# A decoder layer with product-key experts: 24 first-layer tiles beside the gate matrix, 64 in a stage of their own, outputs summed in groups of four

## The chip, the cores and the metric

The program runs on one core of one Trainium2 chip. The metric is the device time of one execution in microseconds (us), the median of the runs; lower is better. The engines of the core are TensorE (PE; PEld is its loading of weights), VectorE (DVE), ScalarE (ACT), GpSimd (POOL) and SyncE (SP). DMA queues are named by the engine that issues them.

## The reference

One inference step of one layer, for 1024 prompt tokens and 32 sample tokens with D = 1024: three mixers (window attention, gated linear attention, attention into a memory), merged by gates, and then the expert layer, which is all that the change touches:

```python
def one_block(xb):                                   # tokens after RMSNorm
    q = (xb @ wq).reshape(P_BLOCK, P_HEADS, 2, half)  # 8 heads
    s1, s2 = q[:, :, 0] @ k1.T, q[:, :, 1] @ k2.T     # 128 keys each
    v1, i1 = top_k(s1, 16); v2, i2 = top_k(s2, 16)
    sc, sel = top_k(v1 + v2 (all pairs), 16)
    eidx = the 16 chosen of i1 * 128 + i2             # of 16384 experts
    gate = softmax(sc)
    hid = einsum('thkd,td->thk', u_tab[eidx], xb)
    return einsum('thk,thkd->td', gelu(hid) * gate, v_tab[eidx])
```

So y = h + sum over 8 x 16 chosen experts of gate * gelu(u . x) * v, in float32.

## The kernel before

Tokens are held transposed, features on the 128 partitions. The first 256 of the 1056 tokens (`TG`) are computed sparsely: for each of the 2 x 128 pairs of a token tile and a choice, GpSimd gathers 128 rows of u (and later of v) by an indirect DMA, and VectorE multiplies and sums (u), or multiplies and adds (v): 512 row jobs. The other 800 tokens (`TD`) are computed densely over all 16384 experts: 128 tiles of 128 experts. For each tile the hidden values are u times x, then GELU, times a gate that is zero for experts that were not chosen, and then v is applied and added to `m.x2`. Each float32 product is made of three float32r products (`exact_product`, L70: high x high, high x low, low x high), so each operand is first rounded by ScalarE (high) and the rest taken by VectorE (low). A tile's 800 tokens are two halves of 400 columns.

The last stages in order:

- `choose_experts` (L1458): queries, scores, the best 16 by VectorE; beside it TensorE already computes the hidden values of 40 of the 128 tiles (`KEPT`), which go to DRAM (`kept`).
- `build_gate_matrix` (L1715): for 100 groups of 8 tokens, the gates of all experts: VectorE makes one-hot rows (`hot2` L1783, `hot1` L1787), GpSimd weights six of the eight tokens (L1800) and ScalarE two (L1828), TensorE multiplies (L1816), ScalarE copies out (L1837), and SyncE stores a block of four groups (32 tokens, 2 MB) to DRAM (L1859). PSUM banks 0 to 3 are used.
- `run_experts` (L1864): 64 groups of two tiles. Groups 0 to 19 use kept hidden values; from group 20 on TensorE computes the hidden values of two tiles (`hidden_products`, L1961, for the group after) and the outputs of two (`output_products`, L1974) in turn. Per group SyncE loads the gates (`x_g`), kept values, v and u; ScalarE and VectorE split them; VectorE weighs (`weigh`, L2083), and adds each of 16 output sums from PSUM to `m.x2` (`add_output`, L2100, L2106). The row jobs (L2123 for u, L2126 for v) stand between in VectorE's order, one per group in the first 19 groups and some 11 in the later ones, with six row buffers for the gathers (L2064).
- `store_output` (L2172).

All orders are written out by hand, as the programs of the engines; semaphores tie them. A `Block` ends when all engines have ended it.

Of the kernel before, what the change touches and what calls it, by code (L numbers as in the profile page):

```python
# [5 lines left out]
F32 = mybir.dt.float32  # L6
# [34 lines left out]
KEPT = 40  # L41
GR = 2
# [1415 lines left out]
def choose_experts(nc, m, d, sem):  # L1458
# [13 lines left out]
    turns[TURNS] = [("u", x) for x in range(e, KEPT)]  # L1472
    jobs = [("q", 0)] + [job for turn in turns for job in turn]
    with ExitStack() as ctx:
# [14 lines left out]
        cand = sb("pcand", [P, NT, TOPK, TOPK])  # L1489
        best = sb("pbest", [P, NT, TOPK])  # L1490
        expo = sb("pexpo", [P, NT, TOPK])
# [11 lines left out]
        with nc.Block() as block:  # L1503
# [75 lines left out]
            def _(act):  # L1579
# [53 lines left out]
                for x in kept_stored:  # L1633
                    act.wait_ge(x, 16 * (KEPT // 2))

# [79 lines left out]
def build_gate_matrix(nc, m, d, sem):  # L1715


    with ExitStack() as ctx:
        def sb(name, shape, dt=F32):
# [8 lines left out]
        out = sb("gm_out", [P, 2, NK, TBG])  # L1728

        turned, t_kept, hot1_made, hot2_made, weighted, last_weighted, used, copied = (  # L1730
            sem(f"gm_{x}") for x in
            ("turned", "kept", "hot1_made", "hot2_made", "weighted", "last_weighted", "used", "copied"))
        stored = [sem("gm_stored0"), sem("gm_stored1")]
        srcs = (m.e1, m.e2, m.gate)
        iota = m.const[:, C_IOTA:C_IOTA + NK]
        turns = [(s, t) for s in range(3) for t in range(GT, NT)]
        with nc.Block() as block:

            @block.tensor
            def _(pe):  # L1740
                for u, (s, t) in enumerate(turns):
                    r = tile_rows(t)
                    if u >= 8:
                        pe.wait_ge(t_kept, u - 7)
                    pe.transpose(m.ps[:, u % 8, 0:r], srcs[s][0:r, t, :],
                                 m.const[0:r, C_ID:C_ID + r]).then_inc(turned, 1)

            @block.scalar
            def _(act):
                for u, (s, t) in enumerate(turns):  # L1750
                    r, a = tile_rows(t), (t - GT) * P
                    act.wait_ge(turned, u + 1)
                    act.copy(turned_in[s][:, a:a + r], m.ps[:, u % 8, 0:r]).then_inc(t_kept, 1)
# [8 lines left out]

        GROUPS = TBG // G8
        BLOCKS = TD // TBG
        with nc.Block() as block:

            def all_groups(eng, group):
                group(0, True, 0)
                group(1, True, 1)
                with eng.Fori(1, TD // G8 // 2) as i:  # L1770
                    group(2 * i, False, 0)
                    group(2 * i + 1, False, 1)


            @block.vector
            def _(dve):
                def group(g, first, q):
                    cols = bass.ds(G8 * g, G8)
                    if not first:
# [5 lines left out]
                    if not first:  # L1785
# [4 lines left out]

                all_groups(dve, group)

            @block.gpsimd
            def _(pool):
                def group(g, first, q):
                    cols = bass.ds(G8 * g, G8 - 2)
                    pool.wait_ge(hot2_made, g + 1)
                    if not first:
# [5 lines left out]
                all_groups(pool, group)  # L1804

# [642 lines left out]
```

## Time and profile before

| | us |
|---|---|
| median of 3 runs (4488.6 to 4491.19) | 4489.08 |
| the profiled execution's own time | 4497.05 |
| its span, first to last instruction | 4495.3 |
| TensorE busy | 3944.2 (88%) |
| VectorE busy | 2847.1 (63%) |
| ScalarE busy | 1203.8 (27%) |
| GpSimd busy | 1113.1 (25%) |

The profile is one execution. Times in it count from the span's start. A busy TensorE is one with a matmul in flight; an engine's idle time costs something only where the others wait for it. The granted clock is a share of TensorE's full 2.4 GHz, so 0.50 is 1.2 GHz.

### The profile page before, as it was taken

To read this page: it belongs to the slowest core of one execution; us is meant where nothing else is said; L and a number is where in the kernel's file an instruction comes from. 1 tells how busy PE (TensorE), PEld (TensorE's weight loads), DVE (VectorE), ACT (ScalarE), POOL (GpSimd) and SP (SyncE) were. 2 spreads that over 40 slices of the span, in tenths; PEclk is the share of its full clock that TensorE was granted. 3 is DMA by queue.
4 is the path that set the end of the run, shared out by engine and by line. 5 is a ranking of instruction groups with operands and counts; after the bars stand their busy time and mean duration, and the time that the engine had idled before them with its cause. 6 is when DMAs were issued, how large, how long until landed. Compare 5 with 4: busy or idle time off the path is not lost. (4 is left out here: it accounts for less than half of the span.)

```text
span 4495.3 us, 58255 instructions
## 1 busy us (share of the span) xinstructions
PE 3944.2 (88%) x21975; PEld 3709.1 (83%) x21975; DVE 2847.1 (63%) x5001; ACT 1203.8 (27%) x1885; POOL 1113.1 (25%) x696
## 2 busy tenths in 40 slices
PE   4799884769999699999766599999999999999998
PEld 2698573558888599999655599999999999999998
DVE  2000345342222368787999788887788888778887
ACT  2112334121111222222588512222222222222221
POOL 0001000000000222222477400144434434334442
PEclk8899876579999799999999899999999999999999
DMA  2211100011112012222233566677777787777775
GB/s 98 59 41 36 58 23 19 21 40 43 43 43 74 30 61 77 74 77 82 84 159 149 213 186 181 190 238 245 244 234 252 253 251 243 239 248 246 246 251 184
DMA packets 366054, 622.15 MB, mean 138 GB/s; under 512 B 224241, under 2 KB 235425, under 8 KB 361907
## 3 DMA queue, kind: packets, MB, share of 16 engines
q1 hardware_dynamic: 285915, 334.56, 23.6%
q0 software_dynamic: 73728, 268.47, 18.1%
q10 hardware_dynamic: 6240, 16.99, 1.0%
q8 instruction: 89, 1.46, 0.1%
q14 instruction: 82, 0.67, 0.0%
HBM read 542.33 MB, written 78.12 MB: 138 GB/s over the span
## 5 line engine op out<-in xcount | busy, mean ns | idle before, releaser
L73 PE MATMUL ps<-x_act_high,x_v_high 128*128 128x400 f32 x2048 | 709.7, 347 | 53.8 <-DVE x_v_low L2080 28.6
L74 PE MATMUL ps<-x_act_low,x_v_high 128*128 128x400 f32 x2048 | 705.2, 344 | 0.0
L75 PE MATMUL ps<-x_act_high,x_v_low 128*128 128x400 f32 x2048 | 704.5, 344 | 0.0
L2106 DVE TENSOR_TENSOR xn<-xn,ps 128x400 f32<-128x400 f32 x1024 | 543.0, 562 | 51.4 <-PE ps L75 51.1
L2064 POOL DMA_INDIRECT x_rows<-in_u_rows,row_of x256 | 326.5, 1275 | 788.3 <-DVE x_row_hid L2123 736.0
L73 PE MATMUL ps<-hd_high,x_u_high 128*128 128x400 f32 x1408 | 484.8, 344 | 0.0
L74 PE MATMUL ps<-hd_low,x_u_high 128*128 128x400 f32 x1408 | 482.9, 343 | 0.0
L75 PE MATMUL ps<-hd_high,x_u_low 128*128 128x400 f32 x1408 | 481.9, 342 | 0.0
L2064 POOL DMA_INDIRECT x_rows<-in_v,row_of x256 | 335.5, 1310 | 472.3 <-DVE xn L2126 426.5
L73 PEld LDWEIGHTS ps<-x_act_high,x_v_high 128*128 128x128 f32 x2048 | 385.6, 188 | 66.0 <-DVE xn L2106 36.9
L74 PEld LDWEIGHTS ps<-x_act_low,x_v_high 128*128 128x128 f32 x2048 | 385.2, 188 | 0.0
L75 PEld LDWEIGHTS ps<-x_act_high,x_v_low 128*128 128x128 f32 x2048 | 384.7, 188 | 0.1
L2126 DVE SCALAR_TENSOR_TENSOR xn<-x_rows,x_row_hid,xn 128x1024 f32<-128x1024 f32 x256 | 328.2, 1282 | 2.3
L73 PE MATMUL ps<-hd_high,wq_high 128*128 128x400 f32 x896 | 309.8, 346 | 17.1 <-ACT kept_act L1597 17.1
L1816 PE MATMUL ps<-gm_wgt,gm_hot 128*128 128x128 f32 x1600 | 206.0, 282 | 134.9 <-ACT gm_out L1837 127.7
L2010 ACT CAST x_v_high<-x_v_raw 128x1024 fp32r<-128x1024 f32 x128 | 132.5, 1049 | 688.3 <-DMA x_v_raw<-in_v 688.3
L1816 PEld LDWEIGHTS ps<-gm_wgt,gm_hot 128*128 128x128 f32 x1600 | 187.6, 193 | 153.2 <-ACT gm_out L1837 148.6
L74 PE MATMUL ps<-hd_low,wq_high 128*128 128x400 f32 x896 | 308.8, 345 | 0.0
L2123 DVE CUSTOM_DVE_ANT_1 x_rows<-x_rows,xn 128x1024 f32<-128x1024 f32 x256 | 307.9, 1218 | 0.0
L75 PE MATMUL ps<-hd_high,wq_low 128*128 128x400 f32 x896 | 307.6, 343 | 0.0
L73 PE MATMUL ps<-x_high_again,w_spare 128*128 128x352 f32 x768 | 269.9, 351 | 38.8 <-DVE x_low L1368 30.5
L2080 DVE TENSOR_TENSOR x_v_low<-x_v_raw,x_v_high 128x1024 fp32r<-128x1024 f32 x128 | 156.3, 1221 | 215.4 <-ACT x_v_high L2010 215.0
(335 smaller groups left out, 7702.0 us busy)
## 6 DMA issues: line engine op xcount, KB each, us to landing
x_v_raw<-in_v SPq DMA_DIRECT2D x128, 512.0 KB, 5.2
gates<-gm_out SPq DMA_DIRECT2D x25, 2048.0 KB, 6.3
x_g<-gates SPq DMA_DIRECT2D x64, 800.0 KB, 8.9
x_u_raw<-in_u SPq DMA_DIRECT2D x88, 512.0 KB, 4.3
wq_raw<-in_u SPq DMA_DIRECT2D x40, 512.0 KB, 3.2
kept<-kept_act ACTq DMA_DIRECT2D x40, 400.0 KB, 2.4
x_act<-kept SPq DMA_DIRECT2D x40, 400.0 KB, 4.2
wg_raw<-in_w_m SPq DMA_DIRECT2D x24, 512.0 KB, 3.6
```

The lines of the kernel that those rows point to most:

```text
L73: pe.matmul(out, w[0], x[0], start=first, stop=False)
L74: pe.matmul(out, w[0], x[1], start=False, stop=False)
L75: return pe.matmul(out, w[1], x[0], start=False, stop=last)
L1816: mm = pe.matmul(m.ps[:, 2 * q + b, i * P:i * P + P], hot1[:, q, 4 * b + i, :], wgt[:, q, 4 * b + i, :], start=True, stop=True)
L2010: sc.copy(v_high[:, g % 2, i], v_raw[:, g % 2, i]).then_inc(v_highs, 1)
L2064: pool.indirect_dma_start(rows[:, s % ROWS, :], None, src, bass.IndirectOffsetOnAxis(ap=m.row_of[:, t, k:k + 1], axis=0)).then_inc(row_loa ...
L2080: dve.tensor_tensor(v_low[:, g % 2, i], v_raw[:, g % 2, i], v_high[:, g % 2, i].bitcast(F32), ALU.subtract).then_inc(v_lows, 1)
L2106: dve.tensor_tensor(dst, dst, m.ps[:, 4 + x % 4, 0:DC], ALU.add).then_inc(added, 1)
L2123: dve.tensor_tensor_reduce(row, row, m.n_rows[t], 1.0, 0.0, ALU.mult, ALU.add, hid[:, t, k:k + 1]).then_inc(row_used, 1)
L2126: dve.scalar_tensor_tensor(m.y_rows[t], row, hid[:, t, k:k + 1], m.y_rows[t], ALU.mult, ALU.add).then_inc(row_used, 1)
```

## The change

The 88 tiles that `run_experts` computed go to two other places, and `run_experts` is replaced. `build_gate_matrix` computes 24 tiles: after each group's eight products TensorE does a quarter of a tile (12 matmuls, PSUM banks 4 to 7), so that a block of four groups holds one tile; u is loaded by SyncE between the stores of the gates, rounded by ScalarE, and its rest is taken by VectorE. The loops there are written out. A new stage `finish_hidden` computes the other 64 tiles, with three buffers for u and four row jobs per tile beside them (256 of 512). A new stage `add_outputs` takes all 128 tiles from DRAM in 32 groups of four: each output sum is accumulated over four tiles in PSUM before VectorE adds it, in eight banks instead of four, and eight row jobs stand in each group. `gather_rows` and `row_job` are the gathers and row jobs of before as functions. The row buffers lie where the choice of experts held its results.

```diff
-KEPT = 40
-GR = 2
+EARLY = 40
+BESIDE = 24
+GR = 4
+ROWS = 6
+ROWS_BESIDE = 4
...
+        u_raw = sb("gm_u_raw", [P, 2, KT, P])
+        u = (sb("gm_u_high", [P, 2, KT, P], F32R), sb("gm_u_low", [P, 2, KT, P], F32R))
+        hid = m.spare[:, 0:2 * TD].rearrange("p (i t) -> p i t", i=2)
...
+            @block.sync
+            def _(sp):
+                for n in range(2):
+                    sp.dma_start(u_raw[:, n], d["u"][EARLY + n]).then_inc(u_loaded[n], 16)
...
+        PER = TBG // G8
+        GROUPS = TD // G8
...
+                def rest_u(n):
+                    dve.wait_ge(u_high, n + 1)
+                    dve.tensor_tensor(u[1][:, n % 2], u_raw[:, n % 2], u[0][:, n % 2].bitcast(F32),
+                                      ALU.subtract).then_inc(u_low, 1)
+                rest_u(0)
+                for g in range(GROUPS):
+                    q, cols = g % 2, slice(G8 * g, G8 * g + G8)
+                    if g >= 2:
                         dve.wait_ge(weighted, g - 1)
                         dve.wait_ge(last_weighted, g - 1)
                     dve.tensor_tensor(hot2[:, q], iota2[:], key2[:, cols].unsqueeze(1).broadcast_to([P, NK, G8]),
                                       ALU.is_equal).then_inc(hot2_made, 1)
+                    if g >= 2:
                         dve.wait_ge(used, 2 * (g - 1))
                     dve.tensor_tensor(hot1[:, q], iota.unsqueeze(1).broadcast_to([P, G8, NK]),
                                       key1[:, cols].unsqueeze(2).broadcast_to([P, G8, NK]),
                                       ALU.is_equal).then_inc(hot1_made, 1)
+                    if g % PER == 1 and g // PER + 1 < BESIDE:
+                        rest_u(g // PER + 1)
...
+                def quarter(n, i):
+                    c = i // 2
+                    a, z = HALVES[c]
+                    if i == 0:
+                        pe.wait_ge(u_low, n + 1)
+                    if i % 2 == 0 and n >= 2:
+                        pe.wait_ge(gelu_done, 2 * (n - 2) + c + 1)
+                    for k in range(4 * (i % 2), 4 * (i % 2) + 4):
+                        mm = exact_product(pe, m.ps[:, 4 + 2 * (n % 2) + c, 0:DC], [x[:, n % 2, k, :] for x in u],
+                                           [x[:, k, a:z] for x in m.hd], k == 0, k == KT - 1)
+                    if i % 2:
+                        mm.then_inc(hidden, 1)
+                for g in range(GROUPS):
+                    q = g % 2
                     pe.wait_ge(hot1_made, g + 1)
                     pe.wait_ge(weighted, g + 1)
                     pe.wait_ge(last_weighted, g + 1)
                     for b in range(2):
+                        if g >= 2:
                             pe.wait_ge(copied, 2 * (g - 2) + b + 1)
                         for i in range(4):
                             mm = pe.matmul(m.ps[:, 2 * q + b, i * P:i * P + P], hot1[:, q, 4 * b + i, :],
                                            wgt[:, q, 4 * b + i, :], start=True, stop=True)
                         mm.then_inc(used, 1)
+                    if g // PER < BESIDE:
+                        quarter(g // PER, g % PER)
...
+                def weigh(g):
                     act.wait_ge(hot2_made, g + 1)
+                    if g >= 2:
+                        act.wait_ge(used, 2 * (g - 1))
                     for i in (G8 - 2, G8 - 1):
+                        ins = act.activation(wgt[:, g % 2, i], hot2[:, g % 2, :, i], ACT.Copy,
+                                             scale=gate[:, G8 * g + i:G8 * g + i + 1])
                     ins.then_inc(last_weighted, 1)
+                def copy_out(g):
+                    blk = g // PER
+                    if g % PER == 0 and blk >= 2:
                         act.wait_ge(stored[blk % 2], 16 * (blk // 2))
+                    for b in range(2):
+                        at = G8 * (g % PER) + 4 * b
+                        act.wait_ge(used, 2 * g + b + 1)
+                        act.copy(out[:, blk % 2, :, at:at + 4].rearrange("p n t -> p t n"),
+                                 m.ps[:, 2 * (g % 2) + b, :].rearrange("p (t n) -> p t n", t=4)).then_inc(copied, 1)
+                def round_u(n):
+                    act.wait_ge(u_loaded[n % 2], 16 * (n // 2 + 1))
+                    if n >= 2:
+                        act.wait_ge(hidden, 2 * (n - 1))
+                    act.copy(u[0][:, n % 2], u_raw[:, n % 2]).then_inc(u_high, 1)
+                def gelu(n, c):
+                    a, z = HALVES[c]
+                    act.wait_ge(hidden, 2 * n + c + 1)
+                    if n >= 2:
+                        act.wait_ge(kept_stored[n % 2], 16 * (n // 2))
+                    act.activation(hid[:, n % 2, a:z], m.ps[:, 4 + 2 * (n % 2) + c, 0:DC], ACT.Gelu).then_inc(gelu_done, 1)
+                def keep(n):
+                    act.wait_ge(gelu_done, 2 * n + 2)
+                    act.dma_start(d["kept"][EARLY + n], hid[:, n % 2]).then_inc(kept_stored[n % 2], 16)
+                round_u(0)
+                weigh(0)
+                for g in range(GROUPS):
+                    n = g // PER
+                    if g + 1 < GROUPS:
+                        weigh(g + 1)
+                    copy_out(g)
+                    if g % PER == 0:
+                        if n + 1 < BESIDE:
+                            round_u(n + 1)
+                        if 1 <= n <= BESIDE:
+                            gelu(n - 1, 1)
+                    if g % PER == 1 and 1 <= n <= BESIDE:
+                        keep(n - 1)
+                    if g % PER == 2 and n < BESIDE:
+                        gelu(n, 0)
+                for x in kept_stored:
+                    act.wait_ge(x, 16 * (BESIDE // 2))
             @block.sync
             def _(sp):
+                for blk in range(TD // TBG):
+                    if 2 <= blk + 1 < BESIDE:
+                        sp.wait_ge(u_low, blk)
+                        sp.dma_start(u_raw[:, (blk + 1) % 2], d["u"][EARLY + blk + 1]).then_inc(u_loaded[(blk + 1) % 2], 16)
+                    sp.wait_ge(copied, 2 * PER * (blk + 1))
                     sp.dma_start(d["gates"][blk], out[:, blk % 2]).then_inc(stored[blk % 2], 16)
...
+def gather_rows(pool, m, d, r, first, upto):
+    for s in range(first, min(upto, len(r.jobs))):
+        kind, t, k = r.jobs[s]
+        if s >= ROWS:
+            pool.wait_ge(r.used, s - ROWS + 1)
...
+def row_job(dve, m, r):
...
+def finish_hidden(nc, m, d, sem, r):
+    FIRST, RING = EARLY + BESIDE, 3
+    COUNT = NK - FIRST
...
+            @block.sync
+            def _(sp):
+                for n in range(COUNT):
+                    if n >= RING:
+                        sp.wait_ge(hidden, 2 * (n - RING) + 2)
+                    sp.dma_start(u_raw[:, n % RING], d["u"][FIRST + n]).then_inc(u_loaded[n % RING], 16)
+            @block.tensor
+            def _(pe):
+                for n in range(COUNT):
+                    pe.wait_ge(u_lows, n + 1)
+                    for c, (a, z) in enumerate(HALVES):
+                        if n >= 4:
+                            pe.wait_ge(gelu_done, 2 * (n - 4) + c + 1)
+                        for k in range(KT):
+                            mm = exact_product(pe, m.ps[:, 2 * (n % 4) + c, 0:DC], [x[:, n % RING, k, :] for x in u],
+                                               [x[:, k, a:z] for x in m.hd], k == 0, k == KT - 1)
+                        mm.then_inc(hidden, 1)
+            @block.scalar
+            def _(act):
+                def round_u(n):
+                    if n < COUNT:
+                        act.wait_ge(u_loaded[n % RING], 16 * (n // RING + 1))
+                        act.copy(u_high[:, n % RING], u_raw[:, n % RING]).then_inc(u_highs, 1)
+                for n in range(RING - 1):
+                    round_u(n)
+                for n in range(COUNT):
+                    round_u(n + RING - 1)
+                    if n >= 2:
+                        act.wait_ge(kept_stored[n % 2], 16 * (n // 2))
+                    for c, (a, z) in enumerate(HALVES):
+                        act.wait_ge(hidden, 2 * n + c + 1)
+                        act.activation(hid[:, n % 2, a:z], m.ps[:, 2 * (n % 4) + c, 0:DC], ACT.Gelu).then_inc(gelu_done, 1)
+                    act.wait_ge(gelu_done, 2 * n + 2)
+                    act.dma_start(d["kept"][FIRST + n], hid[:, n % 2]).then_inc(kept_stored[n % 2], 16)
+                    row_gelus(act, m, r, ROWS_BESIDE * n, ROWS_BESIDE * n + ROWS_BESIDE)
+                for x in kept_stored:
+                    act.wait_ge(x, 16 * (COUNT // 2))
+            @block.gpsimd
+            def _(pool):
+                gather_rows(pool, m, d, r, 0, ROWS_BESIDE * COUNT + ROWS)
+            @block.vector
+            def _(dve):
+                def rest_u(n):
+                    if n < COUNT:
+                        dve.wait_ge(u_highs, n + 1)
+                        dve.tensor_tensor(u_low[:, n % RING], u_raw[:, n % RING], u_high[:, n % RING].bitcast(F32),
+                                          ALU.subtract).then_inc(u_lows, 1)
+                for n in range(RING - 1):
+                    rest_u(n)
+                for n in range(COUNT):
+                    for i in range(ROWS_BESIDE):
+                        row_job(dve, m, r)
+                        if i == 0:
+                            rest_u(n + RING - 1)
...
+def add_outputs(nc, m, d, sem, r):
+    GROUPS = NK // GR
+    OUT = 2 * KT
+    start = r.done
+    left = len(r.jobs) - start
+    upto = [start + left * (g + 1) // GROUPS for g in range(GROUPS)]
...
+            @block.sync
+            def _(sp):
+                def load_gates(g):
+                    if g:
+                        sp.wait_ge(gated, GR * g)
+                    src = bass.AP(tensor=d["gates"].tensor, offset=g * GR * TBG,
+                                  ap=[[NK * TBG, P], [NK * NK * TBG, TD // TBG], [1, GR * TBG]])
+                    sp.dma_start(gates[:].rearrange("p b i t -> p b (i t)"), src).then_inc(g_loaded, 16)
+                for g in range(GROUPS):
+                    load_gates(g)
+                    if g >= 2:
+                        sp.wait_ge(multiplied, OUT * (g - 1))
+                    for n in range(GR * g, GR * g + GR):
+                        sp.dma_start(act_raw[:, g % 2, n % GR], d["kept"][n]).then_inc(a_loaded[n % (2 * GR)], 16)
+                    for n in range(GR * g, GR * g + GR):
+                        sp.dma_start(v_raw[:, g % 2, n % GR], d["v"][n]).then_inc(v_loaded[n % (2 * GR)], 16)
+            @block.tensor
+            def _(pe):
+                def output_products(g, p, first):
+                    for x in range(OUT):
+                        j, (a, z) = x // 2, HALVES[x % 2]
+                        if not (first and x < 8):
+                            pe.wait_ge(added, OUT * g + x - 7)
+                        for i in range(GR):
+                            if x == 0:
+                                pe.wait_ge(act_lows, GR * g + i + 1)
+                                pe.wait_ge(v_lows, GR * g + i + 1)
+                            mm = exact_product(pe, m.ps[:, x % 8, 0:DC], [y[:, p, i, j * P:j * P + P] for y in v],
+                                               [y[:, p, i, a:z] for y in split], i == 0, i == GR - 1)
+                        mm.then_inc(multiplied, 1)
+                output_products(0, 0, True)
+                with pe.Fori(0, (GROUPS - 2) // 2) as i:
+                    output_products(2 * i + 1, 1, False)
+                    output_products(2 * i + 2, 0, False)
+                output_products(GROUPS - 1, 1, False)
+            @block.scalar
+            def _(sc):
...
+                for g in range(GROUPS):
+                    for n in range(GR * g, GR * g + GR):
+                        round_act(n)
+                    for n in range(GR * g, GR * g + GR):
+                        round_v(n)
+                    if g:
+                        row_gelus(sc, m, r, upto[g - 2] if g >= 2 else start, upto[g - 1])
+            @block.gpsimd
+            def _(pool):
+                gather_rows(pool, m, d, r, start + ROWS, len(r.jobs))
+            @block.vector
+            def _(dve):
...
+                def add_output(g, x):
+                    j, (a, z) = x // 2, HALVES[x % 2]
+                    dst = m.x2[:, j, TG + a:TG + z]
+                    if g:
+                        dve.wait_ge(added, OUT * (g - 1) + x + 1)
+                    dve.wait_ge(multiplied, OUT * g + x + 1)
+                    dve.tensor_tensor(dst, dst, m.ps[:, x % 8, 0:DC], ALU.add).then_inc(added, 1)
+                for n in range(GR):
+                    weigh(n)
+                for n in range(GR):
+                    rest_act(n)
+                for n in range(GR):
+                    rest_v(n)
+                after = {3: (weigh, 0), 4: (weigh, 1), 5: (weigh, 2), 6: (weigh, 3), 7: (rest_act, 0), 8: (rest_act, 1),
+                         9: (rest_act, 2), 10: (rest_act, 3), 11: (rest_v, 0), 12: (rest_v, 1), 13: (rest_v, 2),
+                         14: (rest_v, 3)}
+                for g in range(GROUPS):
+                    for x in range(OUT):
+                        add_output(g, x)
+                        if x in after and g + 1 < GROUPS:
+                            what, i = after[x]
+                            what(GR * (g + 1) + i)
+                        if (x < 4 or x % 2) and r.done < upto[g]:
+                            row_job(dve, m, r)
+                    while r.done < upto[g]:
+                        row_job(dve, m, r)
+                assert r.done == len(r.jobs)
...
+                r = row_sums(nc, m, sem)
+                finish_hidden(nc, m, d, sem, r)
+            add_outputs(nc, m, d, sem, r)
         store_output(nc, m, d, sem)
```

## Rows read from the trace of the kernel before

**Rows 1.** Stretches: length; PE, PEld, DVE, ACT, POOL busy; clock; DMA share; GB/s.

```profile
2187.00:2535.00 348.00, 205.97 (x1600) 187.56 (x1600) 336.07 (x200) 278.23 (x400) 256.81 (x100) 0.99 0.36 151
2572.00:2890.00 318.00, 318.00 (x1745) 317.98 (x1746) 277.18 (x438) 65.23 (x72) 16.90 (x18) 1.00 0.62 181
2890.00:4482.00 1592.00, 1565.88 (x8547) 1554.02 (x8545) 1300.15 (x1803) 334.01 (x441) 638.28 (x487) 1.00 0.76 240
```

**Rows 2.** One turn of the gate stage in order of time (start, us, engine).

```profile
2302.17 2.05 PE L1816 MATMUL ps<-gm_wgt,gm_hot 128*128 128x128 f32 x16 [1.32 <-ACT gm_out L1837]
...
2302.79 2.55 POOL L1800 TENSOR_TENSOR gm_wgt<-gm_hot,gm_gate 128x768 f32<-128x768 bf16 x1 [0.82 <-DVE gm_hot L1783]
2303.53 1.91 ACT L1837 COPY gm_out<-ps 128x512 f32 x2
2303.58 2.31 DVE L1783 TENSOR_TENSOR gm_hot<-gm_iota,gm_key 128x1024 bf16<-128x1024 bf16 x1
...
2306.15 2.57 POOL L1800 TENSOR_TENSOR gm_wgt<-gm_hot,gm_gate 128x768 f32<-128x768 bf16 x1 [0.81 <-DVE gm_hot L1783]
```

**Rows 3.** Start of the gate stage in order of time.

```profile
2187.04 0.69 DVE L1783 TENSOR_TENSOR gm_hot<-gm_iota,gm_key 128x1024 bf16<-128x1024 bf16 x1 [4.97 <-PEq L1737]
...
2190.62 5.40 PE L1816 MATMUL ps<-gm_wgt,gm_hot 128*128 128x128 f32 x32 [4.40 <-POOL gm_wgt L1800]
```

**Rows 4.** DMA issues of the page: count, KB each, median us to landing.

```profile
gates<-gm_out SPq DMA_DIRECT2D x25, 2048.0 KB, 6.3
...
wq_raw<-in_u SPq DMA_DIRECT2D x40, 512.0 KB, 3.2
kept<-kept_act ACTq DMA_DIRECT2D x40, 400.0 KB, 2.4
...
out_y<-xn SPq DMA_DIRECT2D x1, 3200.0 KB, 10.0
...
out_y_rows<-xn SPq DMA_DIRECT2D x2, 512.0 KB, 11.2
```

**Rows 5.** DMA queue of SyncE from 1700 to 2100: packets, MB, share of 16 engines.

```profile
q1 hardware_dynamic: 5328, 19.40, 14.4%
```

**Rows 6.** Groups of the expert stage, 2536 to 4482: busy us, mean ns.

```profile
L2106 DVE TENSOR_TENSOR xn<-xn,ps 128x400 f32<-128x400 f32 x1024 | 543.0, 562 | 51.4 <-PE ps L75 51.1
...
L2126 DVE SCALAR_TENSOR_TENSOR xn<-x_rows,x_row_hid,xn 128x1024 f32<-128x1024 f32 x256 | 328.2, 1282 | 2.3
...
L2080 DVE TENSOR_TENSOR x_v_low<-x_v_raw,x_v_high 128x1024 fp32r<-128x1024 f32 x128 | 156.3, 1221 | 215.4 <-ACT x_v_high L2010 215.0
L2010 ACT CAST x_v_high<-x_v_raw 128x1024 fp32r<-128x1024 f32 x128 | 132.5, 1049 | 688.3 <-DMA x_v_raw<-in_v 688.3
```

**Rows 7.** Short stretches after gaps of TensorE; the third last number is the clock.

```profile
555.00:556.00 1.00, 0.49 (x1) 0.18 (x2) 0.00 (x0) 0.00 (x0) 0.00 (x0) 0.61 1.03 393
...
2180.00:2181.00 1.00, 0.00 (x0) 0.00 (x0) 0.46 (x2) 0.00 (x0) 0.00 (x0) 0.50 0.00 0
2190.00:2193.00 3.00, 2.38 (x11) 2.41 (x12) 3.00 (x3) 1.15 (x3) 2.37 (x2) 0.50 0.00 0
```

**Rows 8.** TensorE's first matmul after a gap, with its idle time before.

```profile
555.51 1.06 PE L765 MATMUL ps<-sm_k,features 128*32 128x512 f32 x1 [3.15 <-DMA sm_k<-in_mem_k]
...
2181.04 3.47 PE L1745 MATMUL ps<-const,e 128*128 128x128 f32 x14 [4.08 <-PEq L1503]
```

**Rows 9.** Stretches of the expert stage; the last two numbers are DMA share and GB/s.

```profile
2541.00:2551.00 10.00, 0.00 (x0) 0.00 (x0) 3.73 (x4) 1.99 (x3) 1.62 (x2) 0.50 1.03 408
3000.00:4200.00 1200.00, 1180.12 (x6450) 1171.77 (x6449) 981.99 (x1384) 256.28 (x339) 496.00 (x379) 1.00 0.78 246
```

**Rows 10.** Start and end of the expert stage in order of time.

```profile
2534.80 0.37 SPq L1932 DMA_DIRECT2D x_g<-gates  x1
...
2555.64 0.70 PE L73 MATMUL ps<-x_act_high,x_v_high 128*128 128x400 f32 x1 [28.58 <-DVE x_v_low L2080]
...
4481.05 0.57 DVE L2106 TENSOR_TENSOR xn<-xn,ps 128x400 f32<-128x400 f32 x1 [0.52 <-PE ps L75]
```

More of the change, by code:

```diff
@@ L1471, in choose_experts @@
             e += 1
-    turns[TURNS] = [("u", x) for x in range(e, KEPT)]
+    turns[TURNS] = [("u", x) for x in range(e, EARLY)]
     jobs = [("q", 0)] + [job for turn in turns for job in turn]
@@ L1855, in _ @@
+                for x in kept_stored:
+                    act.wait_ge(x, 16 * (BESIDE // 2))
             @block.sync
             def _(sp):
-                for blk in range(BLOCKS):
-                    sp.wait_ge(copied, 2 * GROUPS * (blk + 1))
+                for blk in range(TD // TBG):
[3 more added lines that the diff above has]
+                    sp.wait_ge(copied, 2 * PER * (blk + 1))
@@ L2190, in row_jobs, with row_sums @@
     return jobs + [("v", 0, k) for k in range(NK - 8, NK)] + [("v", 1, k) for k in range(NK)]
+def row_sums(nc, m, sem):
+    r = Mem()
+    r.jobs = row_jobs()
+    r.first_v = [next(s for s, (kind, i, _) in enumerate(r.jobs) if kind == "v" and i == t) for t in range(GT)]
+    r.last_u = [max(s for s, (kind, i, _) in enumerate(r.jobs) if kind == "u" and i == t) for t in range(GT)]
+    r.last_of = [None] * GT
+    r.done = 0
+    r.loaded = [sem(f"row_loaded{i}") for i in range(ROWS)]
+    r.used, r.gelu, r.gated = (sem(f"row_{x}") for x in ("used", "gelu", "gated"))
+    return r
@@ new lines, in row_gelus @@
+def row_gelus(act, m, r, first, upto):
+    for t in range(GT):
+        if first <= r.last_u[t] < upto:
+            act.wait_ge(r.used, r.last_u[t] + 1)
+            act.activation(m.row_hid[:, t], m.row_hid[:, t], ACT.Gelu).then_inc(r.gelu, 1)
+def row_job(dve, m, r):
+    s, hid = r.done, m.row_hid
+    kind, t, k = r.jobs[s]
+    row = m.rows[:, s % ROWS, :].rearrange("p (a c) -> p a c", c=TG)
+    if s in r.first_v:
+        dve.wait_ge(r.gelu, t + 1)
+        dve.tensor_tensor(hid[:, t], hid[:, t], m.row_gate[:, t], ALU.mult).then_inc(r.gated, 1)
+        dve.wait_ge(r.gated, t + 1)
+    if r.last_of[t] is not None and kind == "v":
+        dve.wait_ge(r.used, r.last_of[t] + 1)
+    dve.wait_ge(r.loaded[s % ROWS], 16 * (s // ROWS + 1))
+    if kind == "u":
+        dve.tensor_tensor_reduce(row, row, m.n_rows[t], 1.0, 0.0, ALU.mult, ALU.add,
+                                 hid[:, t, k:k + 1]).then_inc(r.used, 1)
+    else:
+        dve.scalar_tensor_tensor(m.y_rows[t], row, hid[:, t, k:k + 1], m.y_rows[t], ALU.mult,
+                                 ALU.add).then_inc(r.used, 1)
+        r.last_of[t] = s
+    r.done += 1
@@ L2411 @@
 }
[L2412 removed]
+SCRATCH = {"skew": (8, P, EXT), "gates": (TD // TBG, NK, NK, TBG), "kept": (NK, P, TD)}
 def declare(nc, arrays):
```

413 lines of the change are left out of this document (86 added, 327 removed).

## The prediction

> **What bounds the kernel now.** I first read the busy time of each engine by stage, because the change touches only the last three stages [rows 1]. While the gate matrix is built (2187 to 2535 us), TensorE is busy 206 of 348 us. In the expert stage behind it TensorE is the bound: 318 of 318 us up to 2890, then 1566 of 1592. So TensorE time there is worth its full length, and 142 us of it lie idle in the gate stage.
>
> The matmul price: 1745 matmuls fill 318.00 us, 0.1822 us each [rows 1]. One tile of first-layer work is 8 x 3 x 2 = 48 matmuls, 8.745 us. One tile of output work is also 48.
>
> Next, what paces the gate stage: one turn of it in time order [rows 2]. A group of eight tokens takes TensorE 2.05 us (16 instructions), yet a turn is 3.36 us, from one weighting of GpSimd to the next. The weighting lasts 2.55 us; VectorE's `hot2`, which takes 0.69 us when GpSimd is idle [rows 3], is drawn out to 2.31 us beside it and ends 0.55 us behind it (2305.89 after 2305.34); the next weighting starts 0.26 us later.
>
> **Part 1: 24 tiles beside the gate matrix.** 24 x 8.745 = 209.9 us leave the TensorE-bound stage. In the gate stage a group becomes 2.05 + 12 x 0.1822 = 4.24 us of TensorE, 16.96 us for a block of four, longer than the four turns' 13.4. If nothing else bound, the stage would grow by 24 x (16.96 - 13.44) = 84 us only.
>
> Something else does bind. Per block, SyncE issues the 2 MB store of the gates and right behind it, on the same queue, the load of the next block's u. The store takes 6.3 us to land; a 512 KB load with nothing ahead of it 3.2 us [rows 4]. What a load does behind a store is seen at the end of the kernel: the two 512 KB stores behind the 3.2 MB one land 11.2 us after their issue, about a transfer each behind the 10.0 us of the first, so a queue is served in order [rows 4]. A 512 KB load costs 14.4% of 400 us over 38 loads = 1.52 us of the DMA engines [rows 5] (the window holds 29 u loads and 9 query loads). So u lands 6.3 + 1.55 = 7.9 us after a block's last copy. Bounds: 3.2 us (no queueing) and 6.3 + 3.2 = 9.5 (it starts when the store has landed); the row of the two stores is nearest to 7.9.
>
> Who waits? ScalarE's `round_u(n+1)` stands in its program right behind the copies of a block's first group, and VectorE's `rest_u(n+1)` behind the second group's `hot1`. Both are in-order, so behind them wait `weigh`, `hot2` of the third group, GpSimd's weighting and TensorE. The next block's u is issued only after this block's last copy, so this is a closed ring: u lands 7.9; round 1.05 and rest 1.2 (1024 columns, as for v [rows 6]); `hot2` alone 0.69 [rows 3]; weighting 2.55 and 0.2 of hand-overs; TensorE's third group 2.05, its quarter 2.19, fourth group 2.05; until the second bank of it is copied 1.2 more (two copies take 1.91 from the first bank's end [rows 2]). Sum 21.1 us for a block, against 16.96. TensorE idles for 21.1 - 17.0 = 4.1 us in each.
>
> That idling has its own price. An idle stretch of 3.15 us left the clock at half (0.61 in the microsecond of the restart), one of 4.08 us too (0.50 before its end) [rows 7, 8]. After a restart the clock stays at 0.50 for about 3 us, and the first two gate groups took 5.40 us instead of 2 x 2.05 [rows 3, 7]: 1.3 us more, and the third group lies on the ring. Ends: 0 (the clock stays) to 1.6. I take 1.4, since 4.1 us is as long as the longer of the two gaps that lost the clock: 22.5 us a block. The Trainium skill, TensorE: Matmul & The Clock Gate, section "HAM oscillation", speaks against this change: short bursts of matmuls with a DMA wait between them fall back to the slow clock at every wait. The rows agree so far; by that rule the result is the 4472 below, without it 22 x 1.4 = 31 us less, 4441.
>
> The ring holds for blocks 1 to 22. Block 0 has its loads early (17.6, its second weighting 0.6 late), block 23 loads none (17.0), block 24 has no tiles (3 x 3.36 and 3.3 to its last copy); ahead stand 5.7 us (round, rest, `hot2`, weighting, hand-overs), behind 6.6 (last store, next stage). Sum: 5.7 + 17.6 + 495.0 + 17.0 + 13.4 + 6.6 = 555.3 us against 2534.8 - 2187.0 = 347.8. The gate stage loses 207.5, about all of the 209.9 that it takes over.
>
> VectorE's 24 rests and ScalarE's 24 rounds, 48 GELUs and 24 store issues add some 4 us to a block on ScalarE and VectorE together; they fit into the 22.5 and cost nothing beyond the ring. The loop written out costs nothing that the trace shows: the stage before it is written out too.
>
> **Part 2: 64 tiles in a stage of their own.** TensorE: 64 x 8.745 = 559.7 us. Under it VectorE has four row jobs and a rest, at most 4 x 1.28 + 1.22 = 6.3 of 8.75 us [rows 6]. A tile moves four gathers, one u load (512 KB each) and a 400 KB store: 3.03 MB in 8.745 us = 347 GB/s, 40% above the 246 GB/s that the expert stage moved at a DMA share of 0.78 [rows 9]. That would be 315 GB/s at a full share, 9.62 us a tile. But 408 GB/s were moved over 10 us while gathers, v and u loads ran together [rows 9]; at that rate 7.43 us. The mix is nearest to the 408, which is of the same gathers and loads: u is asked for two tiles ahead (17.5 us) and six gathers are in flight. I take 5 us of waiting in all; ends 0 and 64 x 0.88 = 56. Around it: first u 4.5, round and rest 2.3, hand-overs 0.4, half clock 1.5 at the start; last GELUs 1 and the wait for the last stores 2.4 [rows 4], stage change 1. Sum 559.7 + 13.1 + 5 = 577.8.
>
> **Part 3: outputs in groups of four.** The 128 output tiles stay 6144 matmuls, 1119.4 us. What goes is half of VectorE's additions: 512 x 0.562 = 288 us [rows 6], but that was beside a TensorE that stood still for 26 of 1592 us only; what can be won is that and the start. VectorE per group of four: 16 x 0.56 + 8 x 0.95 (L2080's by columns) + 4 x 1.22 + 8 x 1.28 = 31.7 of TensorE's 35.0 us, and eight banks let it lag by 17 us, so I expect next to no waiting: 3 us (ends 0 and 32 x 1 us). The start is paid again: on one queue come the gates (1.6 MB: 4.0 us at 408 GB/s, 10 by the 3.2 MB store; 5.5 taken), four activation tiles (1.2 each) and four v (1.52 each), landing 1.7 behind; the first v lands at 13.5, round, rest and the hand-overs put the first matmul at 16, the fourth v 5 us later holds up the first sum: 20 us lost (18 to 26), and 1 for the clock. Before, the first matmul came at 2555.64, 20.8 us after the stage began [rows 10]. Sum 1119.4 + 20 + 1 + 3 + 0.6 (last addition starts) = 1144.
>
> **Sum.** After: 555.3 + 577.8 + 1144 = 2277.1 us from the gate stage's start to the last addition. Before: 4481.05 - 2187.0 = 2294.0 [rows 3, 10], of which 1946.3 lie behind the gates: 10368 x 0.1822 = 1889 and 57 of stalls. So 17 us less; the profiled span goes from 4495.3 to 4478. The profiled execution's own 4497.05 stands 8 above the median of the runs; I carry the difference over: 4489.08 - 17 = 4472.
>
> **The rivals.**
> *The moved tiles are hidden* (u is not held up by the store, or lands by 4.5 us): a block takes 17.6 to 18, 22 x 4.5 to 4.9 less, 4364 to 4373. For it: the idle 142 us. Against it: the order in the queue [rows 4]. 0.09.
> *The ring without the clock's fall*: 21.1 a block, 4441. For it: the clock is 0.99 over the stage now; against it the falls after gaps as long [rows 7, 8]. 0.17.
> *The tile stage is bound by DMA*, the case on the other side: at 9.62 us a tile 4523; it decides from 9.23 us a tile (328 GB/s), where the result is 4498. For it: 315 GB/s at a full share; against: 408. 0.18.
> *VectorE holds up the output stage*: 1 us at each of 32 group borders, 4501. Its slack there is about 2 us. 0.06.
> *The forecast*: 0.50, own range 4455 to 4492.
>
> **How the numbers follow.** The forecast's middle lies 8 us under the bound of "faster" (0.2% is 9 us, about what a measurement of this kernel can tell from no change, so below 4480). Of its 0.50 I give 0.34 to faster, 0.15 to same, 0.01 to slower. With the hidden case 0.09 and the ring without the clock's fall 0.17, faster has 0.60. Same: 0.15 and 0.03 of the DMA case, 0.18. Slower: the rest of the DMA case, VectorE's and 0.01, 0.22. The range from 4420 to 4530 leaves out the hidden case and a tail of the DMA case.
>
> **What would show it.** In the gate stage: a block of 22.5 us, one idle stretch of TensorE of 4 us in each, ended by GpSimd's weighting; ScalarE's rounds of u waiting for the DMA; the granted clock at 0.50 behind it; a stage of 555 us. In the tile stage: 8.75 to 9.0 us a tile, DMA share above 0.9. In the output stage: 35 us a group and TensorE at 99% after its first 20 us. It is wrong if a block takes 17 or 18 us, if a tile takes over 9.2, or if TensorE waits for VectorE at every group border.

## The result, and the profile after

The changed kernel takes 4512.38 us (4506.96 to 4519.28) against 4489.08 (4488.6 to 4494.72) for the kernel before on the same chip: a ratio of 1.0038 (interval 1.0025 to 1.0051; the medians alone are 23.3 us, 0.5%, apart), slower by 0.4% where 0.4% faster was forecast. Its profiled execution took 4512.93 us, with a span of 4511.1.

The stages of the kernel after, in the columns of [rows 1]: gate stage, tile stage, the change to the outputs, output stage.

```profile
2192.00:2779.00 587.00, 444.27 (x2752) 436.53 (x2752) 331.04 (x224) 328.56 (x473) 276.75 (x100) 0.86 0.34 126
2788.00:3352.00 564.00, 558.87 (x3066) 558.45 (x3064) 373.03 (x515) 119.88 (x190) 328.24 (x257) 1.00 0.95 345
3352.00:3376.00 24.00, 0.32 (x1) 0.35 (x2) 9.15 (x10) 7.41 (x8) 0.00 (x0) 0.50 0.84 275
3400.00:4490.00 1090.00, 1090.00 (x5993) 1089.92 (x5992) 923.88 (x1174) 218.61 (x242) 229.83 (x245) 1.00 0.79 266
```

Behind the gates all is as forecast: TensorE full for 1090 of 1090 us of outputs, 99% busy in the tile stage with DMA at 0.95 of its share. The gate stage is not: TensorE idle for 143 of 587 us, at a granted clock of 0.86 instead of 0.99. The page's slices say the same at a glance (the gate stage is slices 20 to 25):

```profile
PE   4799884769999699999777777999979999999998
...
PEclk8899776589999799999888888999989999999999
```

The stages' borders, in order of time: the first gate store and the one 22 blocks later lie 528.79 us apart (2215.87, 2744.66), **24.04 us a block** where 22.5 was forecast. Then the tile stage and the output stage begin.

```profile
2215.87 0.33 SPq L1912 DMA_DIRECT2D gates<-gm_out  x1
...
2779.53 17.91 SPq L2018 DMA_DIRECT2D h_u_raw<-in_u  x4
...
3356.26 0.38 SPq L2113 DMA_DIRECT2D x_g<-gates  x1
```

One block of the kernel after, from one store to the next, in order of time (it is the ring that was forecast, all its links in the forecast order):

```profile
2407.40 0.33 SPq L1912 DMA_DIRECT2D gates<-gm_out  x1
...
2407.77 0.43 SPq L1910 DMA_DIRECT2D gm_u_raw<-in_u  x1
...
2415.92 1.05 ACT L1873 CAST gm_u_high<-gm_u_raw 128x1024 fp32r<-128x1024 f32 x1 [4.56 <-DMA gm_u_raw<-in_u]
2417.00 1.23 DVE L1785 TENSOR_TENSOR gm_u_low<-gm_u_raw,gm_u_high 128x1024 fp32r<-128x1024 f32 x1 [9.56 <-ACT gm_u_high L1873]
...
2418.14 0.68 DVE L1795 TENSOR_TENSOR gm_hot<-gm_iota,gm_key 128x1024 bf16<-128x1024 bf16 x1
...
2418.91 2.73 POOL L1812 TENSOR_TENSOR gm_wgt<-gm_hot,gm_gate 128x768 f32<-128x768 bf16 x1 [9.76 <-DVE gm_hot L1795]
...
2421.74 3.75 PE L1841 MATMUL ps<-gm_wgt,gm_hot 128*128 128x128 f32 x16 [5.43 <-POOL gm_wgt L1812]
...
2427.87 1.95 PE L1841 MATMUL ps<-gm_wgt,gm_hot 128*128 128x128 f32 x16
...
2431.02 0.33 SPq L1912 DMA_DIRECT2D gates<-gm_out  x1
```

Link by link, in this block, then as the mean of the 22 blocks from the same rows of each, then (in brackets) as forecast: store to round of u 8.52, mean 8.84 (7.9); round, rest and `hot2` up to the weighting 2.99, 2.98 (2.94); weighting and hand-over 2.83, 2.83 (2.75); third group and its quarter 6.13, 6.23 (2.05 + 2.19 + 1.4 for the clock = 5.64); fourth group to the next store 3.15, 3.16 (3.25). Together 23.62, 24.04 (22.5). So of the 1.5 us too little, 0.94 is u's landing and 0.59 the clock. u's landing varies: about 8.5 us in sixteen blocks and 9.2 to 10.2 in six, of which these lines show the latest. Why those six are late is not shown.

```profile
2335.47 0.33 SPq L1912 DMA_DIRECT2D gates<-gm_out  x1
...
2345.62 1.04 ACT L1873 CAST gm_u_high<-gm_u_raw 128x1024 fp32r<-128x1024 f32 x1 [6.17 <-DMA gm_u_raw<-in_u]
```

The waits from 2200 to 2770 (engine, line, waited for: us in total, times, longest) show the chain behind u: ScalarE waits for the DMA 22 times, VectorE for ScalarE, GpSimd for VectorE, TensorE for GpSimd.

```profile
POOL gm_wgt L1812 <- DVE gm_hot L1795: 256.6, 72, 11.4
DVE gm_u_low L1785 <- ACT gm_u_high L1873: 221.0, 23, 11.2
...
PE ps L1841 <- POOL gm_wgt L1812: 129.5, 24, 7.0
ACT gm_u_high L1873 <- DMA gm_u_raw<-in_u: 108.0, 22, 6.2
```

The rows for the clock, around that restart of TensorE at 2421.74 (columns of [rows 1]): 0.91 on the mean of the ten microseconds before, which end in the idle stretch of 5.43 us, and 0.50 (1.2 GHz) in the five behind.

```profile
2411.00:2421.00 10.00, 5.31 (x36) 4.98 (x34) 4.00 (x4) 3.95 (x7) 2.09 (x1) 0.91 0.51 173
2421.00:2424.00 3.00, 2.26 (x10) 2.29 (x11) 3.00 (x3) 1.71 (x4) 2.37 (x2) 0.50 0.02 5
2424.00:2426.00 2.00, 2.00 (x10) 1.99 (x10) 2.00 (x2) 1.36 (x2) 1.37 (x2) 0.50 0.00 0
```

### The profile page after: what moved, and what is told of

Same layout as the page of the kernel before. It is cut to its first block and busy times, and to the rows that moved or that the text cites. A ratio compares the mean times of both kernels' runs of the same rounds, so it can differ in the third digit from the quotient of the medians.

```text
span 4511.1 us, 55275 instructions
## 1 busy us (share of the span) xinstructions
PE 3962.7 (88%) x21975; PEld 3747.5 (83%) x21975; DVE 2576.3 (57%) x4489; ACT 1200.6 (27%) x1885; POOL 1038.6 (23%) x696
## 5 line engine op out<-in xcount | busy, mean ns | idle before, releaser
L1958 POOL DMA_INDIRECT rows<-in_v,row_of x256 | 244.9, 956 | 757.5 <-DVE xn L1987 725.5
L1958 POOL DMA_INDIRECT rows<-in_u_rows,row_of x256 | 324.7, 1268 | 372.6 <-DVE row_hid L1984 316.6
L2200 DVE TENSOR_TENSOR xn<-xn,ps 128x400 f32<-128x400 f32 x512 | 290.5, 567 | 175.5 <-PE ps L78 175.4
L76 PE MATMUL ps<-hd_high,h_u_high 128*128 128x400 f32 x1024 | 353.9, 346 | 13.7 <-DVE h_u_low L2063 13.7
L1812 POOL TENSOR_TENSOR gm_wgt<-gm_hot,gm_gate 128x768 f32<-128x768 bf16 x100 | 276.7, 2767 | 335.8 <-DVE gm_hot L1795 294.1
L77 PE MATMUL ps<-hd_low,h_u_high 128*128 128x400 f32 x1024 | 352.4, 344 | 0.0
L78 PE MATMUL ps<-hd_high,h_u_low 128*128 128x400 f32 x1024 | 351.5, 343 | 0.0
L2153 ACT CAST x_act_high<-x_act_raw 128x800 fp32r<-128x800 f32 x128 | 110.4, 863 | 861.5 <-DVE x_act_raw L2180 861.2
L1987 DVE SCALAR_TENSOR_TENSOR xn<-rows,row_hid,xn 128x1024 f32<-128x1024 f32 x256 | 328.1, 1282 | 2.0 <-DMA rows<-in_v,row_of 2.0
L1984 DVE CUSTOM_DVE_ANT_1 rows<-rows,xn 128x1024 f32<-128x1024 f32 x256 | 304.9, 1219 | 3.6 <-DMA rows<-in_u_rows,row_of 3.6
```

Source lines behind the costliest of these rows:

```text
L76: pe.matmul(out, w[0], x[0], start=first, stop=False)
L77: pe.matmul(out, w[0], x[1], start=False, stop=False)
L78: return pe.matmul(out, w[1], x[0], start=False, stop=last)
L1812: pool.tensor_tensor(wgt[:, q, 0:G8 - 2], hot2[:, q, :, 0:G8 - 2].rearrange("p n t -> p t n"), gate[:, cols].unsqueeze(2).broadcast_to([P, ...
L1958: pool.indirect_dma_start(m.rows[:, s % ROWS, :], None, src, bass.IndirectOffsetOnAxis(ap=m.row_of[:, t, k:k + 1], axis=0)).then_inc(r.loa ...
L1984: dve.tensor_tensor_reduce(row, row, m.n_rows[t], 1.0, 0.0, ALU.mult, ALU.add, hid[:, t, k:k + 1]).then_inc(r.used, 1)
```

## The experiments

The theory: a block is a ring through u's late landing, and the clock's fall behind each wait adds to it. Its rivals: GpSimd, VectorE or TensorE itself has no room for a quarter of a tile beside a group, so that the block would be as long with u in time; or the loss lies in the new tile stage, and tiles beside the gates are well placed. Ratios are to the kernel before, run in the same job: 4494.52 us for the first four, 4494.84 for the last two, which ran on another chip. Beside the change itself it had taken 4489.08, so a difference to the change's 4512.4 is known to some 5 us only.

**u one block earlier.** There are two buffers of u; the changed kernel asks for u(n+1) after block n-1's last copy, though the buffer is free much earlier, as soon as VectorE has taken the rest of u(n-1). At the same place, still behind the store of block n-1, SyncE now asks for u(n+2) instead of u(n+1).

```diff
                 for blk in range(TD // TBG):
-                    if 2 <= blk + 1 < BESIDE:
-                        sp.wait_ge(u_low, blk)
-                        sp.dma_start(u_raw[:, (blk + 1) % 2], d["u"][EARLY + blk + 1]).then_inc(u_loaded[(blk + 1) % 2], 16)
+                    if blk + 2 < BESIDE:
+                        sp.wait_ge(u_low, blk + 1)
+                        sp.dma_start(u_raw[:, blk % 2], d["u"][EARLY + blk + 2]).then_inc(u_loaded[blk % 2], 16)
                     sp.wait_ge(copied, 2 * PER * (blk + 1))
```

> In the changed kernel a block of the gate stage takes 24.0 us (22 blocks from 2215.9 to 2744.7). Theory 'ring': it is that long because u is asked for only at the block's start and behind the 2 MB store, so that rounds, rests and weighting wait for it. Here u is asked for one block earlier, with the same buffers. The ring is then open and TensorE binds with 3.97 us a turn, 16 to 17 us a block: 22 x 7 to 8 us less, 4340 to 4360. Rival 'in-order work': the added rounds, rests and GELUs on ScalarE and VectorE hold the turns up by themselves, 19 to 20 us a block, about 4415 to 4430. Rival 'not u': the block stays at 23 to 24 us and the time above 4495.

Measured: 4348.62 us (4348.53 to 4350.35), ratio 0.9682 (0.9662 to 0.9702). Its gate stage and the middle of its tile stage, in the columns of [rows 1]:

```profile
2192.00:2616.00 424.00, 396.58 (x2752) 389.07 (x2752) 325.81 (x221) 329.49 (x470) 274.77 (x100) 0.99 0.46 175
2640.00:3170.00 530.00, 530.00 (x2917) 529.99 (x2916) 358.13 (x493) 115.96 (x184) 309.53 (x242) 1.00 0.96 346
```

TensorE is busy 94% of that window, at a clock of 0.99, and the stage is 159 us shorter (429.0 instead of 588.0); a block takes 16.81 us (2211.96 to 2565.03 over 21), TensorE's own 16.96 of the forecast. u still lands 8.2 us after its issue, and nobody waits for it. So no engine lacked room; the whole loss came from asking for u a block too late, and with that undone the change is worth 3.2%.

**u first, at the same moment.** Only the order of the two transfers is turned round: the same u as in the change is asked for at the same moment, right after a block's last copy, but ahead of that block's store and not behind it.

```diff
                 for blk in range(TD // TBG):
-                    if 2 <= blk + 1 < BESIDE:
-                        sp.wait_ge(u_low, blk)
-                        sp.dma_start(u_raw[:, (blk + 1) % 2], d["u"][EARLY + blk + 1]).then_inc(u_loaded[(blk + 1) % 2], 16)
                     sp.wait_ge(copied, 2 * PER * (blk + 1))
+                    if blk + 2 < BESIDE:
+                        sp.wait_ge(u_low, blk + 1)
+                        sp.dma_start(u_raw[:, blk % 2], d["u"][EARLY + blk + 2]).then_inc(u_loaded[blk % 2], 16)
                     sp.dma_start(d["gates"][blk], out[:, blk % 2]).then_inc(stored[blk % 2], 16)
```

> u is issued at the same moment as in the changed kernel (after the block's last copy), but ahead of the store on the queue instead of behind it. Theory 'queue order': u lands some 4 us after the copy instead of 8.5, TensorE's idle stretch shrinks under 1 us and the clock stays: 17 to 17.5 us a block, 4360 to 4375. Rival 'late issue': what matters is that u is asked for only after the last copy, and the store's packets, which follow at once, share the DMA engines: u lands at 6 to 7 us, 20 to 22 us a block, 4425 to 4465.

Measured: 4365.43 us (4360.81 to 4369.68), ratio 0.9718 (0.9696 to 0.974); a block takes 17.50 us. Its DMA issues (count, KB each, median us to landing) against those of the kernel after, which follow:

```profile
gates<-gm_out SPq DMA_DIRECT2D x25, 2048.0 KB, 9.0
...
gm_u_raw<-in_u SPq DMA_DIRECT2D x24, 512.0 KB, 4.4
```

```profile
gates<-gm_out SPq DMA_DIRECT2D x25, 2048.0 KB, 7.2
...
gm_u_raw<-in_u SPq DMA_DIRECT2D x24, 512.0 KB, 8.1
```

Ahead of the store u lands in 4.4 us instead of 8.1, and ScalarE's waits for it shrink from 108.0 us in all to 11.3. So it is the 2 MB ahead of it on the queue that made u late. The store lands 1.8 us later by it (9.0 against 7.2), and nothing waits for that. The ring is still closed: its links, as means of the 22 blocks (u 4.06, then 2.99, 2.84, 4.05 and 3.55), add up to the block's 17.5. So issuing early beats issuing first by 16.8 us.

**The clock kept up.** Late u stays; 22 matmuls a block, into a bank whose GELU is done, are put into TensorE's idle stretch. Their results are never read, so this kernel computes 484 matmuls more than the change and the same outputs.

```diff
+WARM = 22
...
                     if g // PER < BESIDE:
                         quarter(g // PER, g % PER)
+                    n = g // PER
+                    if g % PER == 1 and 1 <= n < BESIDE - 1:
+                        pe.wait_ge(gelu_done, 2 * (n - 1) + 1)
+                        for k in range(WARM):
+                            pe.matmul(m.ps[:, 4 + 2 * ((n - 1) % 2), 0:DC], u[0][:, n % 2, k % KT, :],
+                                      m.hd[0][:, k % KT, 0:DC], start=True, stop=True)
```

> The changed kernel with 22 matmuls without use in each of 22 blocks, in TensorE's idle stretch in front of the third group, into a PSUM bank that is free then; nothing else is changed. Theory 'the clock's fall is on the ring': third group and quarter take 6.1 us after the idle stretch at half clock instead of 4.0 to 4.2; with the clock kept the block takes 22 us, 22 x 1.9 = 42 us less, about 4470. Rival 'the clock's fall is hidden': no change, 4505 to 4520, or slower if the matmuls without use reach into the third group.

Measured: 4471.83 us (4464.61 to 4475.88), ratio 0.9951 (0.9934 to 0.9967), 40.6 us under the change. Its gate stage, and the third and fourth group of two blocks, one behind the other, in order of time:

```profile
2192.00:2735.00 543.00, 493.47 (x3233) 485.73 (x3232) 323.56 (x220) 330.06 (x470) 272.58 (x99) 0.97 0.36 137
```

```profile
2377.80 2.74 PE L1842 MATMUL ps<-gm_wgt,gm_hot 128*128 128x128 f32 x16 [2.33 <-POOL gm_wgt L1813]
...
2383.43 1.95 PE L1842 MATMUL ps<-gm_wgt,gm_hot 128*128 128x128 f32 x16
...
2401.12 2.02 PE L1842 MATMUL ps<-gm_wgt,gm_hot 128*128 128x128 f32 x16 [1.57 <-POOL gm_wgt L1813]
...
2405.17 1.95 PE L1842 MATMUL ps<-gm_wgt,gm_hot 128*128 128x128 f32 x16
```

In the second of these blocks the third group takes 2.02 us where it took 3.75, and with its quarter 4.05, where the change takes 6.23 on the mean. So the clock's fall costs 2.2 us a block, not 1.4. In sixteen of the 22 blocks the clock was held like this, and a block takes 21.7 us. In the other six, the first block above among them, TensorE still idled for 2.2 to 3.1 us, third group and quarter take 5.4 to 5.7 us and the block 24.0; in five of these six u had come more than 9.3 us after the store. (One block idled for 2.2 us and kept the clock.) The mean block of 22.3 us is 1.7 below the change's, and 22 x 1.7 = 37 us are most of the 40.6. Useless work of TensorE made the kernel faster. The wait for u, which the first experiment removes, is the larger part by far.

**No tile beside the gates.** All 88 tiles go to the tile stage, the gate stage is that of before, the outputs are those of the change.

```diff
-BESIDE = 24
+BESIDE = 0
...
-                for n in range(2):
+                for n in range(min(2, BESIDE)):
...
-                rest_u(0)
+                if BESIDE:
+                    rest_u(0)
...
-                round_u(0)
+                if BESIDE:
+                    round_u(0)
...
-                        if 1 <= n <= BESIDE:
+                        if BESIDE and 1 <= n <= BESIDE:
...
-                for x in kept_stored:
+                for x in kept_stored if BESIDE else []:
```

> No tile beside the gate matrix: all 88 in the tile stage, with 352 row jobs there and 160 in the output stage. The gate stage is as before the change but with its loops written out. By the traces: gate stage 348 us instead of 588, tile stage 88 x 8.745 + 15 = 785 instead of 577, output stage 1141 as now: 32 us less than the changed kernel, 4480, about 9 less than before the change. Rival 'writing out the gate stage's loops costs': the gate stage takes 20 us or more above 348. Rival 'the tile stage can't carry 88': over 8.9 us a tile.

Measured: 4477.79 us (4471.78 to 4478.67), ratio 0.9964 (0.9953 to 0.9975). Its gate, tile and output stage, in the columns of [rows 1]:

```profile
2187.00:2535.00 348.00, 203.75 (x1601) 187.64 (x1600) 335.19 (x200) 277.72 (x403) 273.70 (x100) 0.98 0.36 151
2535.00:3321.00 786.00, 770.67 (x4224) 770.23 (x4224) 519.50 (x685) 171.03 (x266) 443.97 (x358) 0.99 0.96 344
3321.00:4461.00 1140.00, 1120.61 (x6144) 1119.30 (x6144) 854.47 (x1069) 232.09 (x257) 144.24 (x154) 0.99 0.65 222
```

By the forecast's own terms this kernel was 88 x 8.745 + 13.1 + 5 = 788 us of tiles and 1144 of outputs; it took 786 and 1140. So the parts behind the gates win 17 us together, and the 24 tiles beside the gates lose 34.6 (4512.4 - 4477.8; some 32 by the gate and tile stages of the two traces) as the change places them. With u in time the same 24 tiles win 129.2 us (4477.8 - 4348.6), which is 24 x (8.745 - (16.81 - 13.44)) = 129.

**Does DMA bind the tile stage?** From here on the base is the kernel with u early. A fifth gather for each tile goes to the tile stage (and leaves the output stage).

```diff
-ROWS_BESIDE = 4
+ROWS_BESIDE = 5
```

> The kernel of e1_u_early with five row jobs per tile in the tile stage instead of four (320 of the 512 there, 192 in the output stage). A tile then moves 3.56 MB, 407 GB/s at TensorE's 8.745 us. Theory '408': what was moved for 10 us at the start of the old expert stage can be moved here too; the tile stays under 8.9 us and the time at 4349 (4345 to 4360). Rival 'nearly full': the tile stage moved 345 GB/s at a DMA share of 0.95, so 363 is the limit: 9.8 us a tile, 64 x 1.06 = 68 us more, about 4417.

Measured: 4361.67 us (4358.38 to 4364.39), ratio 0.9704 (0.9688 to 0.9721), 13 us more than with four: 1.7 us above what the first theory gave, and 55 below its rival. The middle of its tile stage:

```profile
2640.00:3170.00 530.00, 523.97 (x2864) 521.37 (x2864) 427.82 (x569) 113.49 (x182) 382.95 (x294) 1.00 1.01 394
```

394 GB/s over 530 us, with TensorE still busy 99% of it. The whole stage grew by 20 us, from 575.5 to 595.5, of which this window's idling is 6; some 11 lie at the stage's end (TensorE idle for 20 of the 40 us from 3170 here, for 8.5 of the 22 us from 3170 with four), 3 were not followed. With four gathers the stage asks for 346 GB/s, well below: it is bound by TensorE. The rival that took 315 GB/s from [rows 9] as the limit is out.

**Outputs in pairs again.** Groups of two tiles instead of four in the output stage, the jobs on rows spread over the group as before.

```diff
-GR = 4
+GR = 2
...
-                after = {3: (weigh, 0), 4: (weigh, 1), 5: (weigh, 2), 6: (weigh, 3), 7: (rest_act, 0), 8: (rest_act, 1),
-                         9: (rest_act, 2), 10: (rest_act, 3), 11: (rest_v, 0), 12: (rest_v, 1), 13: (rest_v, 2),
-                         14: (rest_v, 3)}
+                after = {3: (weigh, 0), 5: (weigh, 1), 7: (rest_act, 0), 9: (rest_act, 1), 11: (rest_v, 0),
+                         13: (rest_v, 1)}
```

> The kernel of e1_u_early with output groups of two tiles instead of four (64 groups, 1024 additions instead of 512, four row jobs a group), all else the same. Theory 'additions count now': by durations VectorE has 16 x 0.567 + 4 x 0.98 + 2 x 1.22 + 4 x 1.28 = 20.6 us for 17.5 us of TensorE, some 19 with the overlap seen in the output stage (945 us busy against 1014 by durations); VectorE becomes the bound and the time 80 to 130 us longer, 4430 to 4480. Rival 'additions are hidden either way', as the prediction put it (only the standing still of 26 us and the start are to be won): 4350 to 4380.

Measured: 4407.13 us (4402.11 to 4411.07), ratio 0.9809 (0.9792 to 0.9825), 58.5 us more than with fours, between the ranges of the two theories. The middle of its output stage and, from its waits, the largest of TensorE:

```profile
3230.00:4350.00 1120.00, 1073.38 (x5814) 1054.73 (x5813) 1113.86 (x1633) 221.44 (x245) 229.02 (x242) 1.00 0.84 259
```

```profile
PE ps L76 <- DVE x_v_low L2191: 46.6, 60, 1.2
```

VectorE is busy 1113.86 of 1120 us and TensorE waits for it. So VectorE is the bound, as the first theory had it, but a pair takes 18.5 us (96 matmuls of 5814 in 1120 us) and not the expected 19, so the loss is smaller than its 80 to 130. In fours, in the kernel after, VectorE is busy 924 of 1090 us and TensorE is full. So the groups of four keep VectorE off the bound.

## Why the prediction was wrong

- **The step that failed is the block of the gate stage, "22.5 us a block".** Its mechanism was right in each link (u behind the store, ScalarE, VectorE, GpSimd, TensorE, the clock), and each is in the trace after. Its size was off by 1.5 us, 24.04 measured, and it counts 22 times: 34 us. That is nearly all of the 33 us by which the profiled span of 4511.1 missed the forecast 4478: gate stage 588.0 instead of 555.3 (+32.7), tile stage 576.7 instead of 577.8, outputs 3 less than 1144, and 4.5 us more ahead of the gates. Those 4.5 are scatter: the kernel with u early has the same code there and begins its gate stage at 2187.6, 0.6 us after the kernel before.
- **Which terms of the block.** u landed 8.84 us after the last copy on the mean, not 7.9. The forecast took the store's own 6.3 us of [rows 4] and put the load behind it; but with a load behind it the store itself lands in 7.2, so the two overlap, and in six blocks u came about 1.1 us later still, which stays open. The clock's fall cost 2.2 us (6.23 against 4.05 with the clock held, third experiment), not 1.4, and lies outside the ends of 0 to 1.6 that the forecast gave it: the wait was 5.4 us rather than 4.1, and the half clock lasted for at least the 4.3 us from 2421.74 to 2426, past the third group and into its quarter, where [rows 7] had given some 3. The other links are each within 0.1 us.
- **The sum was the difference of two large terms.** 207.5 us lost against 209.9 won left the parts behind the gates to give the sign. An error of 7% in a term that counts 22 times was worth twice the forecast gain. The time lies 20 us above the forecast's own range of 4455 to 4492. The whole range, up to 4530, held it only by the room given to the rival bound by DMA, which did not come true: that was luck. A chance of 0.22 for slower was too low, since only 0.01 of it stood for a ring a microsecond longer than forecast.
- **The 8 us carried over.** Profiled execution minus median was 8 us for the kernel before and 0.5 for the kernel after. In later runs the kernel before had a median of 4494.5, with single runs from 4485 to 4504, so that difference was scatter between executions and no property to carry over.
- **The rivals.** That the tiles are hidden does not hold for the change, but is what it becomes with u early: 4348.6, somewhat below the 4364 that this rival gave. The ring without the clock's fall does not hold either: the fall costs 22 x 2.2 = 48 us (31 forecast), and where the third experiment held the clock a block took 21.7 us, close to that rival's 21.1. The trace after agrees with the Trainium skill, TensorE: Matmul & The Clock Gate, section "HAM oscillation", by which a TensorE that waits a few microseconds for a DMA between its bursts restarts at the slow clock each time: the clock is 0.50 behind the wait, and third group and quarter take over 5.4 us in all 22 blocks. The tile stage is not bound by DMA (fifth), and VectorE does not hold up the outputs (TensorE 1090 of 1090).
- **Tile and output stage** came within 1 and 3 us. One sentence there was incomplete: of the additions saved "what can be won is that [26 us] and the start" compares with the old layout; in the new one pairs would have cost 58.5 us.

The version with u asked for one block earlier beats both kernels: 4348.6 us, 3.2% under the kernel before and 3.6% under the change.

## What to carry to other kernels

When work is put beside a stage that seems to have room, follow its loads to their place in the queue: a small load issued behind a large store arrives after it, and through engines that work in order that delay came back to the next store and became the pace of the stage. Ask for an operand as soon as its buffer is free, not when the loop comes round to it. And when a forecast is a small difference of large terms, carry the error of each term times its count into the chances, not only into the range.

## What was unexpected

Filling TensorE's wait with 22 useless matmuls a block won 40.6 us of 4512, because the idle stretch of 5.4 us had left the clock at half for over 4 us of needed work; and it held the clock in sixteen of 22 blocks only. And two transfers on one queue are not simply one after the other: the 2 MB store took 6.3 us to land alone, 7.2 with a 512 KB load behind it and 9.0 with the load ahead; a 512 KB load took 3.2 with no store on the queue, 4.4 ahead and 8.1 behind. Nor did the DMA share of one stage tell what another can move: 246 GB/s at 0.78 in the old expert stage [rows 9] make 315 at a full share, and here 394 GB/s stood at 1.01.
